# Seven block products in place of eight in the query/key and second gate projections of a two-block transformer kernel

## The chip, the cores and the metric

The kernel runs on one core of a Trainium2 chip, as one program. The metric is the device time of one execution in microseconds, the median over runs. A core has a matrix engine (TensorE, "PE"), a vector engine (VectorE, "DVE"), an activation engine (ScalarE, "ACT"), GpSimd ("POOL") and SyncE ("SP"), which here issues nearly all DMAs, in order, from one queue. All data is float32 unless a row says bf16.

## The reference

256 tokens of width 1024 pass a Conformer/SSM block with a convolutional FFN, and then a second block: adaptive RMSNorm, one input projection, two attentions, two gates, and a mixture of 32 experts. What the change touches is the second block's input projection and its users:

```python
h = rmsnorm(x, norm1_g[l]) * (1.0 + sc1[:, None, :]) + sh1[:, None, :]
proj = h @ w_in[l]
q_m, k_m, v_m, q_d, k_d, v_d, gate_m, gate_d = jnp.split(proj, IN_SPLITS, axis=-1)
qm = apply_rope(to_heads(q_m, MOBA_HEADS, MOBA_HEAD_DIM), cos_m, sin_m)   # k_m, q_d, k_d alike
...
merged = jax.nn.sigmoid(gate_m) * y_m + jax.nn.sigmoid(gate_d) * y_d
x = x + g1[:, None, :] * (merged @ w_out[l])
...
y_ffn = hierarchical_moe(h2, ...)        # 32 experts of 1024x512, 1024x512, 512x1024
```

q_m, k_m, q_d, k_d have 512 columns each (2048 together) and gate_m, gate_d 1024 each (2048 together). The other projections stay as they are.

## The kernel before

Weights stream from HBM in units of 512 columns (2 MB) into two buffers `dense[0]`, `dense[1]`, each used by turns (unit n goes to `dense[n % 2]`). A unit may be loaded once the unit two places before it is used up. PSUM has 8 banks; four of them (`NB = 4`) take the tiles of the projections in turn. A tile is 256 output columns for 256 tokens and fills a bank. PE opens a tile only when the tile four places before it has been read (`open_tile`, semaphore `tile_read`). The whole order is written out by hand: each engine has its own program, with semaphores between them, and an instruction that waits holds everything behind it on its engine.

The stages that matter here, in order:

1. FFN down, 8 units of 128 columns over 22 row chunks (L1019). SP loads the units one or two ahead of PE, with the last pieces of `w_ada` (L505), which DVE multiplies and sums.
2. Two norms (`norm("n2")`, `norm("r1")`). At the end DVE scales and ACT adds the bias chunk by chunk (`hT`, L1558), and PE follows the chunks. `keep_on` puts idle matmuls into the gaps.
3. The query/key stage ("qk"), 4 units, 8 tiles. A tile is 16 matmuls of 128x256 (2 halves of 128 columns, 8 chunks of 128 rows), all by `tile` (L769). ACT reads a tile with four copies of 32 partitions (rotated halves, L1565) and one whole copy (L1567). DVE then applies the rotary tables with three operations (L2177 to L2180).
4. The value stage ("v"), 2 units, 4 tiles (L1034).
5. Attention with the gate projection ("gate2", 4 units, 8 tiles) as filling: a loop of 16 steps `a`. A step has the scores of a pair of heads (L1048, in every odd step, issued ahead of the gate matmuls), 6 gate matmuls (L1096), three transposes of the probabilities (L1064), 2 gate matmuls, and after every odd step the products with v (L1081). DVE has `maxima(a + 1)` (L2141 to L2146) and `finish(a)` (L2152, L2156), ACT has `soften` (the exponential, L1576) and `move` (L1586, L1591). For an odd `a` below 8 the transposes wait for finish(a), which on DVE stands behind maxima(a + 1), which waits for the scores of this step.
6. A sum of squares (L1106), two output projections and `out2` (L769), routing, and the experts: 16 pairs, weights in a ring of nine 2 MB slots. Where a slot is still in use SP waits for its release. The first loads for the experts stand in SP's program between those of the projections.

A matmul of float32 is two records in the trace, so 16 matmuls are 32 records.

## Time and profile before

| | |
|---|---|
| median of 3 runs | 1346.85 us (1345.8 to 1349.13) |
| profiled execution, own time | 1348.95 us |
| its span | 1347.1 us |
| PE busy | 1319.4 us (98%) |
| DVE, ACT, POOL busy | 637.0, 270.8, 58.9 us |
| HBM read | 348.82 MB, 260 GB/s over the span |

How to read it: PE is busy almost always, so the first look is for stretches in which PE waits, and for what the wait is. The DMA engines are full in the last third only. Busy time of PE is modelled: matmuls overlap, so the length of a stretch of them is read from start to start, not from the mean duration. Lines are those of the kernel before.

### The profile page before, as it was taken

Reading aid. Unit: us, or ns where it says so; the run is one execution under the profiler, and the core shown is the slowest. Engines: PE = TensorE matmul, PEld = TensorE weight load, DVE = VectorE, ACT = ScalarE, POOL = GpSimd, SP = SyncE. Lnnn points to the kernel's source line nnn. Section 1 sums busy time; section 2 is a strip of 40 time slices with the busy share of each in tenths; the row PEclk is TensorE's granted clock in tenths of the full one; section 3 lists DMA queues with packets and bytes.
Section 4 is the critical chain, followed back from the end, with each engine's and each line's share of the span. In section 5 each row is a group of like instructions: output and inputs, shape, how many; then the busy total and the mean of one; then the engine's idle time right before and its main releaser. Section 6 shows DMA issues by size and latency. Waiting matters only on the chain.

```text
span 1347.1 us, 18147 instructions
## 1 busy us (share of the span) xinstructions
PE 1319.4 (98%) x6910; PEld 918.0 (68%) x6910; DVE 637.0 (47%) x1384; ACT 270.8 (20%) x566; POOL 58.9 (4%) x60
## 2 busy tenths in 40 slices
PE   9999999999999999999899999999999999999997
PEld 6888888888899888888685788854333433443332
DVE  4652389998426776720531455244333333332322
ACT  2311133220203000100442431033111111112112
POOL 0002112000000111100000000000000000000001
PEclk9999999999999999999999999999999999999999
DMA  7345333343447988767553344569999999999995
GB/s 270 126 153 160 108 126 127 126 141 125 167 146 267 323 300 308 228 192 262 226 181 131 126 188 168 207 227 414 419 423 427 427 428 428 427 427 428 425 422 218
DMA packets 122219, 350.93 MB, mean 261 GB/s; under 512 B 4768, under 2 KB 66464, under 8 KB 108704
## 3 DMA queue, kind: packets, MB, share of 16 engines
q1 hardware_dynamic: 120528, 348.68, 67.9%
q10 hardware_dynamic: 1616, 1.20, 0.3%
q8 instruction: 52, 0.85, 0.3%
q14 instruction: 23, 0.19, 0.0%
HBM read 348.82 MB, written 1.05 MB: 260 GB/s over the span
## 4 chain that ended last, share of the span: by engine, by line
PE 82%; DMA 7%; DVE 6%; issue 2%; ACT 1%; DVEq 1%; POOLq 0%; POOL 0%; SPq 0%; ACTq 0%
PE bank L769 38%; PE bank L1216 20%; PE bank L1019 6%; DMA arena<-in_w_gate 4%; PE bank L1096 4%; PE bank L1188 3%; PE bank L1306 2%; DVE arena L1881 2%; DMA dense<-in_w_gate 2%; PE bank L1034 2%; DVE scratch L1895 1%; PE bank L983 1%; PE bank L971 1%; PE bank L1048 1%; PE bank L822 0%
## 5 line engine op out<-in xcount | busy, mean ns | idle before, releaser
L769 PE MATMUL bank<-hT,dense 128*128 128x256 f32 x2048 | 446.0, 380 | 1.3 <-ACT hT L1407 0.8
L769 PEld LDWEIGHTS bank<-hT,dense 128*128 128x128 f32 x2048 | 388.5, 190 | 57.7 <-issue 6.3
L1216 PE MATMUL bank<-arena,scratch 128*64 128x512 f32 x864 | 228.0, 599 | 6.1 <-DMA arena<-in_w_gate 5.7
L1216 PEld LDWEIGHTS bank<-arena,scratch 128*64 128x64 f32 x864 | 71.0, 138 | 130.6 <-issue 118.5
L769 PE MATMUL bank<-arena,dense 128*128 128x256 f32 x704 | 154.6, 381 | 0.4 <-DVE arena L1957 0.4
L769 PEld LDWEIGHTS bank<-arena,dense 128*128 128x128 f32 x704 | 134.4, 191 | 20.1 <-issue 2.0
L1881 DVE SCALAR_TENSOR_TENSOR arena<-arena,par 128x256 f32<-128x256 f32 x240 | 97.8, 485 | 0.0
L2349 DVE TENSOR_TENSOR scratch<-scratch,bank 128x512 f32<-128x512 f32 x64 | 41.2, 684 | 92.1 <-PE bank L1306 90.7
L1216 PE MATMUL bank<-arena,hT 128*64 128x512 f32 x336 | 78.0, 596 | 0.7 <-ACT hT L1667 0.7
L1019 PE MATMUL bank<-region,dense 128*128 128x256 f32 x352 | 76.1, 379 | 0.0
L1019 PEld LDWEIGHTS bank<-region,dense 128*128 128x128 f32 x352 | 67.0, 190 | 9.0
L1216 PE MATMUL bank<-dense,scratch 128*64 128x512 f32 x160 | 70.6, 594 | 0.0
L2367 DVE SCALAR_TENSOR_TENSOR resid<-bank,lamp,resid 128x512 f32<-128x512 f32 x32 | 24.0, 750 | 94.3 <-PE bank L1216 94.3
L2056 DVE SCALAR_TENSOR_TENSOR arena<-arena 128x1024 f32<-128x1024 f32 x48 | 61.7, 1338 | 8.4 <-DMA arena<-in_w_ada 4.3
L1096 PE MATMUL bank<-hT,dense 128*128 128x256 f32 x256 | 61.0, 384 | 0.0
L2354 DVE TENSOR_TENSOR hT<-hT,bank 128x512 f32<-128x512 f32 x16 | 11.0, 687 | 99.6 <-PE bank L1216 99.6
L1216 PEld LDWEIGHTS bank<-arena,hT 128*64 128x64 f32 x336 | 24.2, 137 | 41.8 <-issue 40.0
L1096 PEld LDWEIGHTS bank<-hT,dense 128*128 128x128 f32 x256 | 46.6, 190 | 8.5 <-issue 3.3
L1654 ACT ACTIVATE scratch<-bank,small,gs 128x128 f32<-128x128 f32 x128 | 46.4, 474 | 3.9 <-PE bank L1188 3.9
L1663 ACT ACTIVATE hT<-bank 128x512 f32<-128x512 f32 x16 | 9.6, 597 | 181.4 <-PE bank L1216 181.4
L1188 PE MATMUL bank<-stat,region 128*128 128x128 bf16 x672 | 42.1, 219 | 0.0
L1819 DVE SCALAR_TENSOR_TENSOR arena<-bank,par,arena 128x255 f32 (+5 forms) x72 | 34.7, 481 | 9.6 <-DVE arena L1819 5.8
(355 smaller groups left out, 1173.9 us busy)
## 6 DMA issues: line engine op xcount, KB each, us to landing
dense<-in_w_in SPq DMA_DIRECT2D x23, 2048.0 KB, 8.2
arena<-in_w_gate SPq DMA_DIRECT2D x21, 2048.0 KB, 22.4
arena<-in_w_up SPq DMA_DIRECT2D x20, 2048.0 KB, 22.4
arena<-in_w_down SPq DMA_DIRECT2D x17, 2048.0 KB, 24.7
arena<-in_w_ada SPq DMA_DIRECT2D x12, 2048.0 KB, 8.1
dense<-in_w_ffn_up SPq DMA_DIRECT2D x22, 1024.0 KB, 7.7
dense<-in_w_down SPq DMA_DIRECT2D x8, 2048.0 KB, 28.9
arena<-in_w_up SPq DMA_DIRECT2D x14, 1024.0 KB, 23.7
```

Source lines behind the costliest of these rows:

```text
L769: last = mm(dst, chunk(k, m), src[:, k, :], start=k == 0, stop=k == k_n - 1)
L1019: last = mm(dst, w[:, k, :], act_t[:, k, :], start=k == 0, stop=k == KF - 1)
L1034: last = mm(b[:], hT[:, k, c * P:(c + 1) * P], w[:, k, :], start=k == 0, stop=k == KD - 1)
L1096: last = mm(b[:, m, :], w[:, k, (a % 4) * P:(a % 4 + 1) * P], hT[:, k, :], start=k == 0, stop=k == KD - 1)
L1188: last = mm(bank[m // 4][:, (m % 4) * 2 * CAP:(m % 4 + 1) * 2 * CAP], x[:, c, m * P:(m + 1) * P], s[:, r, c * 2 * CAP:(c + 1) * 2 * CAP], ...
L1216: last = mm(dst[e * CAP:(e + 1) * CAP, :], tokens(k, e), w[e][:, k, :], start=k == 0, stop=k == k_n - 1)
L1306: ins = mm(spread_bank[2 * half + c][:], selT[:, r, c * P:(c + 1) * P], x, start=n == 0, stop=n == 2)
L1654: f(xe[:, r, k * 2 * CAP:(k + 1) * 2 * CAP], bank[k // 4][:, (k % 4) * 2 * CAP:(k % 4 + 1) * 2 * CAP], ACT.Identity, scale=gs2[:, k:k + 1] ...
L1819: ins = stt(xbcT[:, at_j, s:T], src[:, :, 0:T - s], par_at("ssm_w", j * 4 + (3 - s)), xbcT[:, at_j, s:T], ALU.mult, ALU.add)
L1881: stt(conv_o[:, k, :], glu_v[:, k, ds(i, T)], par_at("conv_w", i + k * CK), conv_o[:, k, :], ALU.mult, ALU.add).then_inc(sem_("tap"), 1)
L2056: stt(w[:, m, :], w[:, m, :], 1.0, c_act, ALU.mult, ALU.mult, accum_out=mod[:, ds(turn * 8 + (4 * i + m), 1)]).then_inc(sem_("ada_summed"), 1)
L2349: tt(part, part, spread_bank[q][:], ALU.add).then_inc(sem_("y_added"), 1)
```

## The change

Each qk tile and each gate2 tile (2x2 blocks of the weight: 2 column halves of 128, 2 row halves of 512, and 2 token halves of 128) is computed by the Winograd form of Strassen's scheme: seven products of 4 matmuls of 128x128, 28 in place of 16 of 128x256. The products come in three groups: "first" p1, p3, p5, p6 (16 matmuls), "second" p7, p2 (8), "third" p4 (4), in the order first(t+1), second(t), third(t-1). They need

- sums of weight blocks per tile: 4 operations of 128x512, by DVE for qk (`weight_sums`), by POOL for gate2;
- four token sums of 128x512 once, by DVE after the norm, ahead of everything that DVE did there;
- fixes per tile: ACT copies two of the four products out of the bank (`copy_products`), DVE adds once or twice after each group (`fix_first`, `fix_second`, `fix_third`), and the result stands in the bank again, where ACT reads it as before.

A third weight buffer (slot 6 of the arena) is used for these ten units, so the load of unit n waits for unit n-3. Slots 0 and 1 now hold the sums, so the first two gate matrices of the experts and one down matrix are loaded after the last gate2 tile; the first qk unit is loaded among the FFN down units.

```diff
+FAST0, FAST1 = UNIT["qk"][0], UNIT["gate2"][0] + UNIT["gate2"][1]
+def buffer(n):
+    if FAST0 <= n < FAST1:
+        return (2, FAST0 % 2, 1 - FAST0 % 2)[(n - FAST0) % 3]
+    return n % 2
+SLOTS = {"p1": 0, "p3": 1, "p6": 2, "p5": 3, "p7": 2, "p2": 0, "p4": 2}
+BLOCK = {"first": ("p1", "p3", "p5", "p6"), "second": ("p7", "p2"), "third": ("p4",)}
...
@@ sync
                 load("down", u, lambda t: v3(t[:, 0:KF * P], P), wdn[:, :, u * P:(u + 1) * P])
                 if u < 2:
                     load_ada(10 + u)
+                if u == 1:
+                    load("qk", 0, flat, wi2[:, :, 0:512])
...
-            for e in range(2):
-                load_matrix("gate", e, 0)
-
+            load("qk", 1, flat, wi2[:, :, 512:1024])
+            load("qk", 2, flat, wi2[:, :, 1536:2048])
             sp.wait_ge(sem_("ada_summed"), 48)
             for e in range(2):
                 load_matrix("up", e, 0)
-            for u, c in enumerate((0, 512, 1536, 2048)):
-                load("qk", u, flat, wi2[:, :, c:c + 512])
+            load("qk", 3, flat, wi2[:, :, 2048:2560])
...
+            sp.wait_ge(tile_done, TILE["gate2", 7] + 1)
+            for e in range(2):
+                load_matrix("gate", e, 0)
             load_matrix("down", 1, 0)
@@ gpsimd
+            for t in range(NFAST):
+                n, j, tt = U0("gate2") + t // 2, t % 2, nc.gpsimd.tensor_tensor
...
+                tt(s1, a21, a22, ALU.add).then_inc(sem_("sums_ready"), 1)
+                pool.wait_ge(sem_("sums_ready"), before_t + 1)
+                tt(s2, s1, a11, ALU.subtract).then_inc(sem_("sums_ready"), 1)
+                pool.wait_ge(sem_("sums_ready"), before_t + 2)
+                tt(s4, a12, s2, ALU.subtract).then_inc(sem_("sums_ready"), 1)
+                tt(a21, a11, a21, ALU.subtract).then_inc(sem_("sums_ready"), 1)
@@ tensor
+            def fast(name, t, block, i0=0, i1=None, ready=None):
...
+                    if (block, i) == ("first", 0):
+                        open_tile(name, t)
+                        pe.wait_ge(sem_("sums_ready"), sums_count(name, t))
+                    if block == "second" and i == 0:
+                        pe.wait_ge(sem_("fast_fixed"), fast_count(name, "first", t))
+                    if block == "third" and i == 0:
+                        pe.wait_ge(sem_("fast_fixed"), fast_count(name, "second", t))
...
-            for u in range(4):
-                unit_512("qk", u, hT, ready=None if u else by_chunk("r1_out"))
+            fast("qk", 0, "first", 0, 8, ready=first_tokens)
+            fast("qk", 1, "first", 0, 8)
+            fast("qk", 0, "first", 8, 16, ready=first_tokens)
+            fast("qk", 1, "first", 8, 16)
+            for block, t in ORDER[2:]:
+                fast("qk", t, block)
...
-                some(0, 6)
-                attend(a, lambda: some(6, KD))
+                some(14 * a, 14 * a + 10)
+                attend(a, lambda: some(14 * a + 10, 14 * a + 14))
@@ scalar
+            for t in range(NFAST):
+                copy_products("qk", t)
+                if t >= 3:
+                    read_qk(t - 3)
...
@@ vector
+            for t in range(NFAST):
+                if t == 0:
+                    weight_sums("qk", 2)
+                fix_first("qk", t)
+                if t:
+                    fix_second("qk", t - 1)
+                    if t >= 2:
+                        fix_third("qk", t - 2)
+                    if t + 2 < NFAST:
+                        weight_sums("qk", t + 2)
+                if t == 1:
+                    unscale()
+                if t >= 4:
+                    rope(t - 4)
```

Where instructions stand now. SP's queue at the start of FFN down, before:

```order
L475 DMA dense1<-in_w_ffn_down 128x22x128 [waits tile_done]
L505 DMA arena<-in_w_ada_2 128x4x1024 [waits ada_summed]
L475 DMA dense0<-in_w_ffn_down 128x22x128 [waits tile_done]
L505 DMA arena<-in_w_ada_2 128x4x1024 [waits ada_summed]
L475 DMA dense1<-in_w_ffn_down 128x22x128 [waits down_unit]
L475 DMA dense0<-in_w_ffn_down 128x22x128 [waits tile_done]
```

and now (the last load but one is down unit 2):

```order
L537 DMA dense1<-in_w_ffn_down 128x22x128 [waits tile_done]
L567 DMA arena<-in_w_ada_2 128x4x1024 [waits ada_summed]
L537 DMA dense0<-in_w_ffn_down 128x22x128 [waits tile_done]
L567 DMA arena<-in_w_ada_2 128x4x1024 [waits ada_summed]
L537 DMA arena<-in_w_in_2 128x8x512
L537 DMA dense1<-in_w_ffn_down 128x22x128 [waits down_unit]
L537 DMA dense0<-in_w_ffn_down 128x22x128 [waits tile_done]
```

The first qk unit (`in_w_in_2`) went in front of down unit 2. ACT in the qk stage, before (tiles 0 and 1, in banks 3 and 0):

```order
L1565 ACTIVATE scratch1<-bank3 32x512 [waits tile_done,norm_ssq]
L1565 ACTIVATE scratch1<-bank3 32x512 x3
L1567 ACTIVATE region<-bank3 128x512
L1565 ACTIVATE scratch1<-bank0 32x512 [waits tile_done]
L1565 ACTIVATE scratch1<-bank0 32x512 x3
L1567 ACTIVATE region<-bank0 128x512
```

and now (L1701 is `copy_products` of tiles 0 to 4; bank3 holds tile 0 and then tile 4):

```order
L1701 ACTIVATE arena<-bank3 128x2x128 [waits fast_part,norm_ssq]
L1701 ACTIVATE arena<-bank0 128x2x128 [waits fast_part]
L1701 ACTIVATE region<-bank1 128x2x128 [waits fast_part]
L1701 ACTIVATE arena<-bank2 128x2x128 [waits fast_fixed,fast_part]
L1709 ACTIVATE scratch1<-bank3 32x512 [waits fast_fixed]
L1709 ACTIVATE scratch1<-bank3 32x512 x3
L1711 ACTIVATE region<-bank3 128x512
L1701 ACTIVATE arena<-bank3 128x2x128 [waits fast_fixed,fast_part]
```

The five reads of tile 0 went behind the copy of tile 3. PE in the qk stage, tiles 1 to 4, before (banks 0, 1, 2 and 3):

```order
L769 MATMUL bank0<-hT,dense1 128x256 x15
L769 MATMUL bank1<-hT,dense0 128x256 [waits tile_read1,dense_in0]
L769 MATMUL bank1<-hT,dense0 128x256 x15
L769 MATMUL bank2<-hT,dense0 128x256 [waits tile_read2]
L769 MATMUL bank2<-hT,dense0 128x256 x15
L769 MATMUL bank3<-hT,dense1 128x256 [waits tile_read3,dense_in1]
```

and from the end of tile 3's first group on, now (bank2 tile 3, bank1 tile 2, bank0 tile 1, bank3 tile 4):

```order
L910 MATMUL bank2<-arena 128x128 x8
L910 MATMUL bank1<-arena,dense1 128x128 [waits fast_fixed]
L910 MATMUL bank1<-arena,dense1 128x128 x3
L910 MATMUL bank1<-hT,dense1 128x128 x4
L910 MATMUL bank0<-arena 128x128 [waits fast_fixed]
L910 MATMUL bank0<-arena 128x128 x3
L910 MATMUL bank3<-hT,dense0 128x128 [waits sums_ready,tile_read3]
```

Twelve matmuls (rows two to six) now stand between the end of tile 3's first group and the opening of tile 4's bank; before there was nothing of tile 2 or 1 behind a tile's end, and a bank was opened a whole tile after its last reader could start.

## Rows read from the trace of the kernel before

**Rows 1.** The page: the chain that ended last, by engine.
```profile
PE 82%; DMA 7%; DVE 6%; issue 2%; ACT 1%; DVEq 1%; POOLq 0%; POOL 0%; SPq 0%; ACTq 0%
```
**Rows 2.** Windows: stretch, length, busy us of each engine, PEclk, DMA share, GB/s.
```profile
930.00:1312.00 382.00, 376.44 (x2274) 153.13 (x2272) 124.91 (x249) 61.62 (x155) 0.00 (x0) 1.00 1.01 425
```
**Rows 3.** Waits of PE: total us, times, longest.
```profile
PE bank L1216 <- DMA arena<-in_w_gate: 5.7, 4, 2.1
```
**Rows 4.** Timeline of PE, qk stage and start of v: start us, us, records.
```profile
658.74 55.49 PE L769 MATMUL bank<-hT,dense 128*128 128x256 f32 x256 [0.53 <-ACT hT L1558]
...
714.07 26.34 PE L1034 MATMUL bank<-dense,hT 128*128 128x512 f32 x61
```
**Rows 5.** Chain in order of time: start us, us; 128x128 matmuls, and FFN down.
```profile
416.47 10.50 PE bank L983 x94
...
565.10 75.97 PE bank L1019 x352
```
**Rows 6.** Timeline of SP, FFN down: issue of units 2 and 3.
```profile
574.63 9.86 SPq L475 DMA_DIRECT2D dense<-in_w_ffn_down  x2
```
**Rows 7.** Windows without engines: stretch, length, PEclk, DMA share, GB/s.
```profile
576.00:580.00 4.00, 1.00 1.11 306
580.00:584.00 4.00, 1.00 0.40 99
...
820.00:824.00 4.00, 0.58 1.06 397
```
**Rows 8.** Timeline of PE behind attention.
```profile
818.91 2.82 PE L1106 MATMUL bank<-scratch,con 128*128 128x256 f32 x8 [1.91 <-ACT scratch L1609]
```
**Rows 9.** Timeline of ACT, end of the norm and first qk tile.
```profile
658.09 3.30 ACT L1558 ACTIVATE hT<-hT,small 128x256 f32<-128x256 f32 x8 [2.40 <-DVE hT L2127]
665.98 2.43 ACT L1565 ACTIVATE scratch<-bank 32x512 f32<-32x512 f32 x4 [4.59 <-PE bank L769]
668.43 0.60 ACT L1567 ACTIVATE region<-bank 128x512 f32<-128x512 f32 x1
```
**Rows 10.** Timeline of DVE, the same stretch.
```profile
657.51 3.26 DVE L2127 SCALAR_TENSOR_TENSOR hT<-resid,gs,stat 128x256 f32<-128x256 f32 x8
660.69 1.74 DVE L2130 RECIPROCAL stat<-stat 128x256 f32<-128x256 f32 x1
662.46 2.50 DVE L2132 TENSOR_TENSOR resid<-resid,stat 128x512 f32<-128x512 f32 x4
668.54 0.69 DVE L2177 TENSOR_TENSOR stat<-scratch,con 128x512 f32<-128x512 f32 x1 [3.58 <-ACT scratch L1565]
```
**Rows 11.** Groups by shape: two DVE operations that read PSUM.
```profile
L2015 DVE TENSOR_SCALAR stat<-bank 128x128 f32<-128x128 f32 x2 | 0.6, 292 | 2.9 <-PE bank L993 2.9
L2100 DVE TENSOR_TENSOR resid<-bank,resid 128x256 f32<-128x256 f32 x1 | 0.4, 424 | 9.1 <-PE bank L1019 9.1
```
**Rows 12.** Timeline of PE in attention, steps 0 and 3.
```profile
746.18 0.55 PE L1064 MATMUL bank<-con,scratch 128*128 128x128 f32 x3 [0.84 <-DVE scratch L2156]
...
758.00 2.86 PE L1096 MATMUL bank<-hT,dense 128*128 128x256 f32 x12
760.69 0.49 PE L1064 MATMUL bank<-con,scratch 128*128 128x128 f32 x3
```
**Rows 13.** Timeline of DVE in step 3: end of finish(3).
```profile
759.79 0.67 DVE L2156 TENSOR_SCALAR scratch<-scratch,rsum 128x128 f32<-128x128 f32 x2
```
**Rows 14.** Groups by shape: POOL's operation of 128x512 on SBUF.
```profile
L708 POOL TENSOR_TENSOR arena<-arena 128x512 f32<-128x512 f32 x8 | 10.6, 1348 | 41.0 <-DVE arena L1920 41.0
```
**Rows 15.** Timelines: a DVE operation alone, one beside POOL's, which is last.
```profile
457.91 1.23 DVE L2056 SCALAR_TENSOR_TENSOR arena<-arena 128x1024 f32<-128x1024 f32 x1 [0.47 <-DVE scratch L2044]
459.06 1.74 DVE L2056 SCALAR_TENSOR_TENSOR arena<-arena 128x1024 f32<-128x1024 f32 x1
...
458.30 1.43 POOL L714 TENSOR_TENSOR region<-scratch 128x256 f32 x1 [5.42 <-ACT scratch L1515]
```
**Rows 16.** Timeline of SP behind attention.
```profile
836.44 14.18 SPq L475 DMA_DIRECT2D dense<-in_w_out  x2
```

More of the change, by code:

```diff
@@ L109, with user_before, fast_order, fast_count @@
 UNIT, NUNITS = offsets(UNITS)
+FAST0, FAST1 = UNIT["qk"][0], UNIT["gate2"][0] + UNIT["gate2"][1]
[3 more added lines that the diff above has]
+    return n % 2
+def user_before(n):
+    earlier = [m for m in range(n) if buffer(m) == buffer(n)]
+    return earlier[-1] if earlier else None
+SLOTS = {"p1": 0, "p3": 1, "p6": 2, "p5": 3, "p7": 2, "p2": 0, "p4": 2}
+BLOCK = {"first": ("p1", "p3", "p5", "p6"), "second": ("p7", "p2"), "third": ("p4",)}
+NFAST = 8
+def fast_order():
+    out = [("first", 0)]
+    for t in range(NFAST):
+        if t + 1 < NFAST:
+            out.append(("first", t + 1))
+        out.append(("second", t))
+        if t:
+            out.append(("third", t - 1))
+    return out + [("third", NFAST - 1)]
+ORDER = fast_order()
+FAST_COUNT = {x: i + 1 for i, x in enumerate(ORDER)}
+FAST_TILES = {"qk": 0, "gate2": NFAST}
+def fast_count(name, block, t):
+    return 3 * FAST_TILES[name] + FAST_COUNT[block, t]
+def part_count(name, block, t):
+    return 2 * FAST_TILES[name] + [x for x in ORDER if x[0] != "third"].index((block, t)) + 1
+def sums_count(name, t):
+    return t + (1 if t < 2 else 2) if name == "qk" else NFAST + 1 + 4 * (t + 1)
 HALVES = ("glu", "up")
@@ L159, in program @@
         up_slot, down_slot = [expert[2], expert[3]], [expert[4], expert[5]]
+        bufs = [dense[0][:], dense[1][:], expert[6]]
+        sum_sets = [[v3(arena[:, (3 * i + q) * 512:(3 * i + q + 1) * 512], P) for q in range(3)] for i in range(4)]
+        token_sums = [v3(arena[:, 6144 + 512 * q:6144 + 512 * (q + 1)], P) for q in range(4)]
         wdt = sb("wdt", KD * H)
@@ L1559, in _, with copy_products, read_qk @@
             act.wait_ge(sem_("norm_ssq"), norm_count("r1"))
-            for t in range(8):
-                b = wait_tile(act, "qk", t)
+            def copy_products(name, t):
+                act.wait_ge(sem_("fast_part"), part_count(name, "first", t))
+                if t >= 3:
+                    act.wait_ge(sem_("fast_fixed"), fast_count(name, "third", t - 3))
+                elif name == "gate2":
+                    act.wait_ge(sem_("fast_fixed"), fast_count("qk", "third", NFAST - 1))
+                f(fixes[t % 3][:, 0:4:2, :], v3(bank[TILE[name, t] % NB][:], P)[:, 0:4:3, :], ACT.Copy
+                  ).then_inc(sem_("fast_copied"), 1)
+            def read_qk(t):
+                b = bank[TILE["qk", t] % NB]
+                act.wait_ge(sem_("fast_fixed"), fast_count("qk", "third", t))
                 for to in range(0, P, 32):
@@ L2173, in _, with rope @@
             cos, sin = bc(con("cos"), 2), bc(con("sin"), 2)
-            for t in range(8):
+            def rope(t):
                 dst = qk[:, 2 * t:2 * t + 2, :]
```

184 lines of the change are left out of this document (146 added, 38 removed).

## The prediction

> **What bounds the kernel now.** I read four views, in this order. The chain of waits says that PE holds 82% of what ended last, DMA 7% and DVE 6% [rows 1]. PE's waits say where it isn't PE: the longest cause is the experts' gate matrices, 5.7 us in 4 waits [rows 3]. The windows say why: from 930 to 1312 us the DMA engines are full (share 1.01, 425 GB/s) while PE is at 376.4 of 382 us [rows 2]. So the last third is held by DMA and PE together, and it starts when the out2 tiles release their buffers. It gets neither shorter nor longer by this change, it only moves: a microsecond won or lost ahead of it is a microsecond of the whole. The timelines of the stages in front then show PE without a gap in qk [rows 4] and nearly so in attention, so fewer columns could pay there, one for one, if nothing else comes late.
>
> **What the products save.** The qk stage runs from 658.74 to 714.07, where v starts [rows 4]: 55.33 us for 8 tiles, 6.92 a tile of 16 matmuls. A 128x128 matmul is two records, and 94 such records with a weight load each take 10.50 us [rows 5], 0.2234 us a matmul. A tile of 28 costs 6.26 us, a stage of 8 tiles 50.0 us. That is 5.3 us less in qk and 5.3 us less in gate2.
>
> **qk, the start.** PE takes up the norm's output as ACT writes it, a chunk each 0.41 us until 661.39 [rows 9]. Before, a chunk met a matmul of 0.43 us. Now p1 and p3 want all eight chunks within 8 x 0.22 = 1.8 us and so end near 661.7, not 660.5. Eight matmuls of tile 1 follow, to 663.5; then p5 and p6 want the token sums. DVE is free at 660.77 [rows 10] and has four operations of 128x512 of 0.69 us, with a gap 0.73 each [rows 10], the second behind the last chunk: done near 663.7. PE goes on at 663.9. Together 16 matmuls took 5.1 us in place of 3.6: 1.5 us lost.
>
> **qk, tiles 4 to 7.** This is the step on which most rests. PE may open tile t+1 when ACT has read tile t-3. ACT reads it behind `copy_products(t)`, which waits for the first group of tile t. From the end of this group PE has 8 + 4 matmuls, 2.68 us. ACT needs 0.2 us to see it (a tile's last matmul ends at 658.74 + 6.92 = 665.66, and ACT starts 0.3 later), 0.3 for the copy until the next may start, 3.05 for the five reads of tile t-3 (665.98 to 669.03) [rows 9], and 0.1 back: 3.65 us. So PE waits 0.97 us at each of tiles 4, 5, 6 and 7: 3.9 us. Behind tile 7 the fix of its second group stands on DVE behind a rope of three operations (2.2 us); I count 0.9 us before the last p4. DVE's sum for the stage, by rows: weight sums 2.9 a tile (four of 0.73) for six tiles, fixes 1.9 (two of PSUM 128x256 at 0.42, four of 128x128 at 0.29 [rows 11], with gaps) for eight, the reciprocal and scaling 4.3 [rows 10], four ropes 2.2 each, token sums 2.9: 48.6 us, under PE's 56. The other four ropes go under v, whose 26 us hide them. Stage: -5.3 + 1.5 + 3.9 + 0.9 = +1.0 us. Bounds: -3.8 (only the start is lost) and +4.6 (rival C).
>
> **FFN down.** The first qk unit (2.1 MB) now stands in the queue in front of down unit 2. It has no wait of its own, so it is issued right behind the ada piece and before 574.63, when down unit 2 goes out [rows 6]. Before, the engines were full with the two until about 581.6 (share 1.11, then 0.40 of 4 us) [rows 7]. PE starts unit 2 at 565.10 + 2 x 9.50 = 584.1 [rows 5]: 2.5 us of cover. The new unit takes 2.1 MB / 425 GB/s [rows 2] = 4.9 us, so down 2 lands near 586.7 and PE waits 2.7 us. Later units have their 9.5 us each and no guest. The bounds are 0, and 4.5 at the 306 GB/s of the window before [rows 7]. On order: the Trainium skill, DMA: Bandwidth & Descriptors, "Queues, rings and completion order", says that SP owns one ring on each of the 16 DMA engines and that descriptors in it start in order; by that rule the guest is wholly ahead of down 2, by a fair sharing it would be so only in part. No row here separates the two.
> Does the clock fall? After 1.91 us idle it stood at 0.58 of 2.4 GHz for 4 us, that is mostly at 1.2 GHz [rows 7, 8]: 1.7 us lost. The idle times of up to 2.1 us among the experts left a mean of 1.00 over 382 us [rows 2, 3], so most of those had no fall. I take half, 0.9 us, with bounds 0 and 1.7.
>
> **gate2.** Of the 5.3 us not all arrives. A step has 10 matmuls of 0.223 ahead of the transposes where it had 6 of 0.432: PE comes 0.36 us earlier. In step 0 it already waits 0.84 us for DVE [rows 12]; it waits 0.36 more. In step 3 (and 1, 5, 7, which repeat it) finish(3) ends at 759.79 + 0.67 = 760.46 [rows 13] and the transposes start at 760.69 [rows 12], about 0.1 us after they could; both hang on scores that end at 758.00, so PE comes 0.27 us too early four times: 1.1 us. In even steps DVE has about 2 us of slack, of which the fixes of the odd step before take 1.3. From step 8 on there are 3 us. That leaves 3.8.
> The sums by POOL: 4 operations a tile, 1.35 us each [rows 14], 5.4 us a tile against 9 us of PE. Unit gate2-2 lands some 8 us after v's end and its first use is 31 us after it, so even twice the price is hidden. What is not hidden is what POOL does to DVE: the same operation took 1.74 us beside POOL and 1.23 alone [rows 15]. DVE's critical operations in the odd steps mostly read PSUM or one SBUF tensor; I take 0.4 us (bounds 0 and 4). Gate2 gains 3.4 us. The Trainium skill (GPSIMD Engine Reference, table of figures, "SBUF interfaces") says that POOL's ports are shared with VectorE and contend where DVE has two SBUF inputs; the trace agrees with 1.74 against 1.23.
>
> **Behind attention.** Gate2's last tanh no longer stands between the last product and the square; of its 0.6 us (like L1567 [rows 9]) I count 0.3 won. The idle time of 1.91 us thus becomes 1.6; whether the clock then stays up is open, up to 1.7 us won. I count none. Three matrices (6.3 MB) and down 0 are now loaded here, some 20 us with proj_d, from about 815; out2's load was issued at 836.44 [rows 16] with 14 us to its use at 850.6, so a queue that is full until 840 is hidden by the output projections.
>
> **Sum.** +1.0 +2.7 +0.9 -3.4 -0.3 = +0.9 us. The profiled execution took 1348.95 us for its span of 1347.1, so 1349.85 of its own kind; it lies 2.1 above the median of the runs (1346.85), so 1347.75, say 1347.8.
>
> **Rivals.**
> B, faster: the guest in the DMA queue is hidden (down 2 arrives by 584.1), the clock stays up behind attention, and the transposes aren't early. Then +1.0 - 4.9 (only step 0's 0.4 lost) - 0.3 - 1.7 = -5.9: 1341.0. For it: the cover is 2.5 us and the size of the guest's delay comes from a mean rate. Against: the DMA engines are full when the guest arrives, share 1.11 [rows 7].
> C, slower: DVE becomes the bound of qk. It has 48.6 us of work in 56; some 75 operations, each with a wait on its own semaphore. If each costs 0.15 us more than counted, DVE needs 59.9 and qk grows by 3.6: 1351.4. It decides from 0.1 us more per operation. Against: gaps of dependent operations before are 0.03 to 0.04 us.
> D, slower: in attention, POOL stretches DVE's chain between scores and transposes. If DVE's 2.5 us become 3.0 in all eight first steps, 4 us: 1351.8. It decides from 0.1 us, which is all the slack of the odd steps [rows 12, 13]. Against: POOL is at work in perhaps half of them.
> E, the products don't run at 0.2234 us: they read sums from other places and change groups often. At 0.236, 5.6 us more: 1353.4. Against: the 128x128 rows have loads for each as well.
>
> **Chances.** As forecast 0.50, with its own range 1344 to 1351; B 0.25, C 0.11, D 0.10, E 0.04. 0.3% (4 us) is about what a measurement of this kernel can tell from no change. Below 1342.8 lie most of B and a little of the forecast, 0.22; above 1350.9 most of C, D and E and a little of the forecast, 0.21; the rest, 0.57, between. The range of 1341 to 1354 leaves out a part of B and the case that two of C, D, E meet.
>
> **What would show it.** Four waits of PE of about 1 us each in the qk stage whose releaser is ACT's read (the last of five), and one on DVE before the last p4; a stage of 56 us. A wait of PE of 2 to 3 us on down unit 2, near 584. Waits of 0.2 to 0.4 us for L2156's successor at the transposes of steps 1, 3, 5, 7; an attention stage 3 to 4 us shorter. No wait of PE on POOL's sums, none on out2's weights, and the stretch from the first expert to the end as long as before. I am wrong if qk is under 53 us (ACT's read isn't the limit), if no wait stands near 584, or if the experts' stretch changes its length.

## The result, and the profile after

The changed kernel takes 1364.43 us (median of 4 runs, 1357.15 to 1365.09); the kernel before took 1347.86 us (4 runs) on the same chip. The ratio is 1.011, with a 95% interval of 1.008 to 1.014: slower, by more than the 0.3% that a measurement can tell, and 10 us above the end of the forecast's range. The profiled execution took 1364.54 us, its span 1362.7 us (before 1347.1): 15.6 us to account for.

The page's chain by engine, to be held against [rows 1], shows DVE up from 6% to 8% and ACT from 1% to 3%:

```profile
PE 81%; DVE 8%; DMA 5%; ACT 3%; issue 2%; DVEq 1%; POOLq 0%; POOL 0%; ACTq 0%
```

The window on the experts (stretch, length, busy us of each engine, PEclk, DMA share, GB/s), moved along by 13 us, and their longest wait of PE answer to [rows 2, 3]. The longest wait is 3.6 us where it was 2.1, but the sum is as before, and from the first product of the experts to the end the kernel takes 454.3 us (before 454.5): the loss lies ahead of them.

```profile
943.00:1325.00 382.00, 373.06 (x2258) 152.94 (x2270) 123.00 (x247) 63.14 (x156) 0.00 (x0) 1.00 1.01 424
```
```profile
PE bank L1348 <- DMA arena<-in_w_gate: 5.9, 3, 3.6
```

Three starts of stages (qk, v, the squares), read from the chain of waits, cut the span into parts. In the chain v starts 0.16 us later than in PE's timeline, so that qk before is 55.5 us here and 55.33 in the prediction. "att" is v and attention, up to the eight matmuls on the squares that stand behind attention [rows 8]; "rest" is what follows. All are us of one profiled execution.

```
kernel                          qk starts  qk length   att      rest    span
before                            658.7      55.5     104.7    528.2   1347.1
after                             667.4      57.1     111.9    526.3   1362.7
early unit in the kernel before   664.7      55.5     104.7    526.2   1351.0
unit behind all down units        666.2      57.1     108.8    526.5   1358.6
unit in four parts                658.9      57.1     107.9    526.2   1350.1
GpSimd's sums cut to 8 columns    664.3      57.1     100.4    525.7   1347.5
ScalarE reads first               664.8      54.6     111.9    526.7   1357.9
GpSimd additions in before        660.5      55.5     109.2    527.6   1352.8
sums on VectorE, late             667.5      57.1     117.8    528.0   1370.4
sums on VectorE, early            664.7      57.1     107.3    528.5   1357.6
 and both repairs                 660.5      54.6     109.5    528.1   1352.7
query/key products alone          659.2      54.5     104.7    526.7   1345.1
both repairs, sums released       660.8      54.7     101.5    526.7   1343.7
both repairs, sums not released   660.5      54.7     107.1    525.9   1348.2
```

After against before: +8.6 until qk starts, +1.6 in qk, +7.2 in attention, -1.9 behind it. Each row is one execution; a kernel's executions lie up to 8 us apart (the changed kernel's between 1357 and 1365).

PE's timeline after (start us, us, records, and in brackets the idle time before and what ended it) shows where PE waits. It answers to [rows 4, 8, 12].

```profile
588.00 4.61 PE L1142 MATMUL bank<-region,dense 128*128 128x256 f32 x10 [3.90 <-DMA dense<-in_w_ffn_down]
...
691.31 1.16 PE L910 MATMUL bank<-hT,dense 128*128 128x128 f32 x8 [0.87 <-ACT region L1711]
698.69 1.16 PE L910 MATMUL bank<-hT,dense 128*128 128x128 f32 x8 [0.86 <-ACT region L1711]
706.08 2.05 PE L910 MATMUL bank<-hT,arena 128*128 128x128 f32 x16 [0.87 <-ACT region L1711]
713.47 2.05 PE L910 MATMUL bank<-hT,arena 128*128 128x128 f32 x16 [0.87 <-ACT region L1711]
723.34 1.16 PE L910 MATMUL bank<-arena 128*128 128x128 f32 x8 [0.67 <-DVE arena L2277]
757.46 0.90 PE L1198 MATMUL bank<-con,scratch 128*128 128x128 f32 x3 [2.22 <-DVE scratch L2368]
766.27 0.55 PE L1198 MATMUL bank<-con,scratch 128*128 128x128 f32 x3 [2.50 <-DVE scratch L2368]
777.36 0.55 PE L1198 MATMUL bank<-con,scratch 128*128 128x128 f32 x3 [0.31 <-DVE scratch L2368]
808.49 1.50 PE L1215 MATMUL bank<-scratch,arena 128*128 128x256 f32 x4 [2.54 <-ACT scratch L1742]
836.42 1.99 PE L1238 MATMUL bank<-scratch,con 128*128 128x256 f32 x8 [1.56 <-ACT scratch L1767]
```

The wait at 588 and the qk stage look as forecast. What was not forecast is the size of the waits in attention: 7.6 us in four, where before it was 0.84 in one [rows 12]. The last of the four ends with ACT: its read of the product (L1742) stands behind its exponential, which had waited 7.0 us for DVE's L2358. The windows of 4 us add the clock. Below 1.00 in the third last column some or all of a window ran at 1.2 instead of 2.4 GHz:

```profile
584.00:588.00 4.00, 0.11 (x1) 0.03 (x1) 3.86 (x7) 0.00 (x0) 0.00 (x0) 0.85 1.17 291
588.00:592.00 4.00, 4.00 (x10) 3.20 (x11) 2.27 (x4) 0.00 (x0) 0.00 (x0) 0.50 1.10 274
...
652.00:656.00 4.00, 4.00 (x13) 3.26 (x12) 0.29 (x1) 2.56 (x6) 0.00 (x0) 0.62 1.10 425
756.00:760.00 4.00, 2.54 (x11) 2.32 (x11) 3.03 (x8) 1.22 (x4) 0.94 (x1) 0.68 0.86 318
...
768.00:772.00 4.00, 4.00 (x25) 3.40 (x22) 1.91 (x8) 1.64 (x6) 0.69 (x1) 0.61 0.02 4
808.00:812.00 4.00, 3.51 (x15) 3.34 (x16) 3.55 (x10) 2.41 (x9) 2.86 (x3) 0.58 0.00 0
836.00:840.00 4.00, 3.58 (x17) 3.17 (x18) 1.29 (x2) 3.34 (x6) 0.00 (x0) 1.00 1.06 442
```

Why is DVE late? Its timeline after, at the wait of 2.50 us and ahead of the one of 2.54, and POOL's beside it:

```profile
762.02 0.74 DVE L2357 TENSOR_REDUCE mx<-scratch 128x1 f32<-128x128 f32 x2
762.80 0.61 DVE L2358 TENSOR_SCALAR mx<-mx 128x2 f32<-128x2 f32 x1
...
763.51 2.70 DVE L2368 TENSOR_SCALAR scratch<-scratch,rsum 128x128 f32<-128x128 f32 x2
766.13 0.28 DVE L2268 TENSOR_TENSOR arena<-arena,bank 128x128 f32<-128x128 f32 x1
766.44 1.05 DVE L2270 TENSOR_TENSOR arena<-arena 128x128 f32<-128x128 f32 x1
767.42 0.55 DVE L2353 SCALAR_TENSOR_TENSOR scratch<-bank,con 128x384 f32<-128x384 f32 x1
...
801.54 2.91 DVE L2378 SCALAR_TENSOR_TENSOR scratch<-scratch,rsum 128x128 f32<-128x128 f32 x2
...
805.86 1.19 DVE L2358 TENSOR_SCALAR mx<-mx 128x2 f32<-128x2 f32 x1
```
```profile
762.12 1.27 POOL L806 TENSOR_TENSOR arena<-dense 128x512 f32<-128x512 f32 x1 [5.18 <-PE bank L910]
763.46 1.26 POOL L808 TENSOR_TENSOR arena<-arena,dense 128x512 f32<-128x512 f32 x1
764.80 1.26 POOL L810 TENSOR_TENSOR arena<-dense,arena 128x512 f32<-128x512 f32 x1
766.02 1.32 POOL L811 TENSOR_TENSOR dense<-dense 128x512 f32<-128x512 f32 x1
...
805.75 1.26 POOL L806 TENSOR_TENSOR arena<-arena 128x512 f32<-128x512 f32 x1 [0.17 <-POOL arena L811]
```

The pair that scales the probabilities took 0.67 us before [rows 13]; here 2.70. Its first half takes 1.29 us and ends at 764.80, just behind POOL's second operation (763.46 + 1.26), and its second half takes 1.37 and ends at 766.21, just behind POOL's third (764.80 + 1.26). L2358, two columns that take 0.17 us alone, takes 0.61 and ends at 763.41, POOL's first at 763.39. L2270 ends at 767.49, behind POOL's 767.34. Ahead of the wait at 808 it is the same: L2378 takes 2.91 us for two (0.84 without GpSimd's sums, experiment 3), L2358 1.19 beside POOL's 1.26. DVE's operations that read PSUM (L2268, L2353) or reduce (L2357) keep their times, and POOL's 32 take 1.26 to 1.32 us but for one of 1.46. So DVE is not slowed in proportion: some of its operations end only when POOL's whole operation is over. Of the 24 operations of the pair's line, 20 take 0.28 to 0.35 us and four 1.19 to 1.37, none between.

### The profile page after: what moved, and what is told of

Read it like the earlier page. It is cut to its first block, busy times and chain, and to the rows that moved or that the text cites. A ratio compares the mean times of both kernels' runs of the same rounds, so it can differ in the third digit from the quotient of the medians.

```text
span 1362.7 us, 19122 instructions
## 1 busy us (share of the span) xinstructions
PE 1317.0 (97%) x7279; PEld 929.4 (68%) x7294; DVE 695.9 (51%) x1500; ACT 276.4 (20%) x582; POOL 99.3 (7%) x92
## 4 chain that ended last, share of the span: by engine, by line
PE 81%; DVE 8%; DMA 5%; ACT 3%; issue 2%; DVEq 1%; POOLq 0%; POOL 0%; ACTq 0%
PE bank L858 34%; PE bank L1348 22%; PE bank L910 6%; PE bank L1142 5%; DMA arena<-in_w_gate 4%; PE bank L1320 3%; PE bank L1438 2%; DVE arena L2041 2%; PE bank L1168 2%; DMA dense<-in_w_ffn_down 1%; DVE scratch L2055 1%; PE bank L1106 1%; ACT scratch L1709 1%; PE bank L930 1%; PE bank L1094 1%
## 5 line engine op out<-in xcount | busy, mean ns | idle before, releaser
L858 PE MATMUL bank<-hT,dense 128*128 128x256 f32 x1792 | 390.5, 380 | 0.8 <-ACT hT L1539 0.8
L858 PEld LDWEIGHTS bank<-hT,dense 128*128 128x128 f32 x1792 | 339.3, 190 | 50.5 <-issue 4.9
L1142 PE MATMUL bank<-region,dense 128*128 128x256 f32 x352 | 79.2, 389 | 3.9 <-DMA dense<-in_w_ffn_down 3.9
L910 PE MATMUL bank<-arena 128*128 128x128 f32 x384 | 51.4, 283 | 0.7 <-DVE arena L2277 0.7
L910 PEld LDWEIGHTS bank<-arena 128*128 128x128 f32 x384 | 47.7, 198 | 1.9 <-DVE arena L2277 0.9
L782 POOL TENSOR_TENSOR region<-scratch 128x256 f32 (+1 forms) x22 | 23.2, 1054 | 277.1 <-ACT scratch L1647 277.1
L820 POOL TENSOR_TENSOR hT<-scratch,con 128x512 f32<-128x512 f32 x3 | 3.7, 1270 | 542.2 <-DVE scratch L2594 542.2
```

The lines of the kernel that those rows point to most:

```text
L858: last = mm(dst, chunk(k, m), src[:, k, :], start=k == 0, stop=k == k_n - 1)
L910: last = mm(b[:, SLOTS[p], :], left, right, start=k == 0, stop=k == 3)
L1142: last = mm(dst, w[:, k, :], act_t[:, k, :], start=k == 0, stop=k == KF - 1)
```

## The experiments

Ratios are to the kernel before, run anew beside each group of experiments (medians 1347.3 to 1348.4 us).

**1. The early unit, alone in the kernel before.**

```
+                if u == 1:
+                    sp.dma_start(flat(expert[6]), wi2[:, :, 0:512]).then_inc(sem_("guest_in"), 16)
...
+            sp.wait_ge(sem_("guest_in"), 16)
             load_matrix("down", 1, 0)
```

> The kernel before with one more load: the first query/key unit (2 MB) into an arena slot that is free there, issued by SP behind the last adaptive piece, ahead of FFN down unit 2, where the changed kernel issues it. Nothing else changes (the unit is loaded once more later, as before). Theory G (the early unit delays down unit 2, the PE waits, its clock falls, and the stage and the norm behind it run longer): query/key starts about 8.6 us later than in the kernel before (667.4 instead of 658.7), PE waits 3 to 4 us at about 588 for the down unit, total about 1355 to 1356. Rival N (the unit is absorbed, and the 8.6 us of the changed kernel came from its other instruction order): qk start within 1 us of 658.7, total 1347 to 1348.

Measured: 1352.83 us, ratio 1.0041 (1.0025 to 1.0056). PE's wait on the down unit, and the chain (start us, us, what):

```profile
PE bank L1022 <- DMA dense<-in_w_ffn_down: 3.8, 1, 3.8
```
```profile
574.78 13.17 DMA dense<-in_w_ffn_down
587.95 0.14 issue
588.08 58.90 PE bank L1022 x264
```

Theory G holds, but qk starts 5.9 us later, not 8.6, and the total is under the 1355 expected: 3.8 of waiting, and the six units behind it take 58.9 us instead of 57.0 because the clock falls (0.79 in 584:592). The other 2.7 of the changed kernel are a longer fall at the same place (60.0 us) and a second one in the norm. That one is no property of the change: PE idles 1.9 us there in every kernel, and the clock fell in the profiled executions of some kernels and not of others, whether or not they have the early unit (it did in experiments 5, 10, 11 and 12, and didn't before and in 1, 3, 4, 7, 8 and 9). Of this kernel's +5.9, 2.0 came back behind attention, where the clock stayed up after the same 1.9 us of idle time that it fell after before [rows 7, 8].

**2. The unit behind all down units.**

```
-                if u == 1:
-                    load("qk", 0, flat, wi2[:, :, 0:512])
...
+            load("qk", 0, flat, wi2[:, :, 0:512])
             load("qk", 1, flat, wi2[:, :, 512:1024])
```

> The changed kernel with the load of the first query/key unit moved behind all down units (SP issues it just before the second unit). Theory G: the wait at about 588 goes, query/key starts at 658 to 660 (667.4 in the changed kernel) if the unit is there in time, total 1364.4 - 8.6 = about 1356. Rival L (the unit now comes late for the query/key stage): a wait of PE of 1 us or more on that unit at the stage's start, total 1357 to 1361. Rival N (the order of instructions is the cause): start stays near 667, total 1363 to 1365.

Measured: 1360.98 us, 1.0092 (1.0072 to 1.0112); qk starts at 666.2. None of the three expectations holds as written; L comes nearest, with the total and a unit that is late, but late for DVE. The wait at 588 is gone, but another engine now waits for the unit; DVE's timeline:

```profile
634.94 0.69 DVE L2258 TENSOR_TENSOR arena<-arena 128x512 f32<-128x512 f32 x1 [50.29 <-DMA arena<-in_w_in]
```

`weight_sums("qk", 0)` stands ahead of the residual's additions in DVE's order. The additions start 5.6 us after the unit's arrival, PE waits 3.1 us at 644.6 for the norm's first input, and the clock is at 0.50 from 644 to 652. The unit has a window, then: it may not press on down unit 2, and it must be there by about 631.8, the 3.1 us of PE's wait earlier.

**3. GpSimd's sums cut to almost nothing.** This kernel forms only 8 columns of one plane of each sum of the gate units, so it leaves most of these sums out and its gates are wrong; the number, order and waits of all instructions stay.

```
                 s1, s2, s4 = sum_sets[t % 4]
+                a11, a12, a21, a22, s1, s2, s4 = (x[:, 0:1, 0:8] for x in (a11, a12, a21, a22, s1, s2, s4))
```

> The changed kernel with GpSimd's 32 weight sums of the second branch's gate units cut to 8 columns of one plane of each operand (so nearly all of these sums are left out, and the gates' products run on unsummed data; their number, order and waits stay). Theory C (VectorE's operations on the on-chip memory wait for a whole operation of GpSimd beside them, and PE then waits for VectorE at the probabilities and loses its clock): L2368's TENSOR_SCALAR pair falls back to about 0.67 us each at every head, the waits of 2.22, 2.50 and 2.54 us in the attention go or fall under 1 us, the granted clock in 758:774 and 808:812 rises to 0.9 or more, and the total falls by 7 to 11 us, to 1354 to 1357. Rival F (the fixes and copies of the block products themselves load VectorE and ScalarE too much there): durations fall but the waits stay at 1.5 us or more, total 1361 to 1364.

Measured: 1351.61 us, 1.0030 (1.0017 to 1.0042), so 13 us under the changed kernel, more than the 7 to 11 expected; attention 100.4 us, 11.5 less. The profiled execution also starts qk 3.1 us earlier, which GpSimd's sums can't have done, since they come later: the clock fell less ahead of qk here (58.9 us for the six units behind the wait, not 60.0, and 1.00 in the norm). DVE's groups (line, operation, shapes, count, busy us, mean ns), first here, then in the changed kernel:

```profile
L2369 DVE TENSOR_SCALAR scratch<-scratch,rsum 128x256 f32<-128x256 f32 x12 | 4.2, 353 | 0.4
L2369 DVE TENSOR_SCALAR scratch<-scratch,rsum 128x128 f32<-128x128 f32 x12 | 3.4, 287 | 0.4
```
```profile
L2368 DVE TENSOR_SCALAR scratch<-scratch,rsum 128x128 f32<-128x128 f32 x12 | 6.4, 530 | 0.4
L2368 DVE TENSOR_SCALAR scratch<-scratch,rsum 128x256 f32<-128x256 f32 x12 | 5.3, 438 | 0.4
```

Theory C. PE's waits of 2.22, 2.50, 0.31 and 2.54 shrink to one of 1.2 (step 0, where it was 0.84 before), and no window of attention has a clock under 1.00. The fixes and copies of the block products fit. Against before (104.7), the products themselves save 4.3 us here, 0.5 more than the forecast's 3.8.

**4. ScalarE reads before it copies.**

```
             for t in range(NFAST):
-                copy_products("qk", t)
                 if t >= 3:
                     read_qk(t - 3)
+                copy_products("qk", t)
```

> The changed kernel with ScalarE reading out tile t-3 of query/key before it copies the first products of tile t (now the copy comes first). Theory A (the four waits of 0.87 us in the query/key stage are PE waiting for ScalarE's readout that frees the bank): the four waits go or fall under 0.3 us, the stage shortens by about 3 us (57.1 to 54 us), total about 1361. Rival O (the copy then comes late and the waits move to the arena's or the fix's semaphore): the stage's length stays within 1 us, total 1363 to 1366.

Measured: 1356.43 us, 1.0058 (1.0041 to 1.0075). The four waits of 0.87 become one of 0.3; a new one of 0.8 on DVE's fix (L2268) appears, and and the one before the last p4 grows from 0.67 to 0.94; the stage is 2.6 us shorter (54.6 against 57.1). Theory A, with 0.8 lost again. The median fell by 8.0 us, of which the stage explains 2.6. The profiled execution, the slowest of the four, is 4.8 us under the changed kernel's; beside the stage, qk starts 2.6 us earlier in it, as the clock fell less ahead of it. What the other three won was not traced.

**5. GpSimd additions in the kernel before.** They work on a part of the arena that is free then; one load for the experts goes there later and now stands behind them in SP's queue. What follows attention takes 527.6 us (before 528.2), so this move cost nothing.

```
+            for ready, count in ((1, 8), (4, 4), (6, 4), (10, 8)):
+                pool.wait_ge(sem_("prob_ready"), ready)
+                for _ in range(count):
...
+                    nc.gpsimd.tensor_tensor(z, x, y, ALU.add).then_inc(sem_("extra"), 1)
```

> The kernel before with 24 GpSimd additions of 128x512 on a part of the arena that nothing else uses then (8 from the first probabilities on, 4 from the fourth, 4 from the sixth, 8 from the tenth), one memset ahead of them, and the second-branch experts' load into that part put behind them. VectorE's and TensorE's work is that of the kernel before. Theory C (an operation of VectorE on on-chip memory alone waits for GpSimd's whole operation): L2090s' TENSOR_SCALAR pairs beside GpSimd rise from 0.67 to 1.3 us or more each, PE waits more at the probabilities, and the attention (104.8 us from the first v product to the ossq products) lengthens by 3 to 9 us; total 1350 to 1356. Rival I (the changed kernel's fixes on VectorE are what leaves no slack, GpSimd alone is absorbed): VectorE's operations lengthen but the attention stays within 1.5 us, total 1346.5 to 1349.

Measured: 1354.93 us, 1.0057 (1.0041 to 1.0074); attention 109.2 us instead of 104.7, with every window in it at a clock of 1.00. Here neither products nor fixes are new, PE's work is untouched, and still the pair's means double or more (before 286 and 352 ns) while reductions (before 420) keep theirs, and POOL's operations take what they take elsewhere (1.26 to 1.28 us each). Of the pair's 24 operations 15 take 0.28 to 0.35 us and nine 1.21 to 1.37:

```profile
L2169 DVE TENSOR_SCALAR scratch<-scratch,rsum 128x128 f32<-128x128 f32 x12 | 8.4, 704 | 0.4
L2169 DVE TENSOR_SCALAR scratch<-scratch,rsum 128x256 f32<-128x256 f32 x12 | 8.3, 692 | 0.4
L2158 DVE TENSOR_REDUCE mx<-scratch 128x1 f32<-128x256 f32 x16 | 6.7, 420 | 0.6
```
```profile
L734 POOL TENSOR_TENSOR arena<-arena 128x512 f32<-128x512 f32 x24 | 30.4, 1268 | 55.8 <-DVE scratch L2169 34.5 <-DVE scratch L2179 19.8
```

Theory C again. The Trainium skill (SBUF — State Buffer, "SBUF: two separate sides") calls the port pair of VectorE and GpSimd an exclusive lock, which VectorE needs in a 2-port perf mode or with two SBUF inputs; whichever starts first holds it for its whole instruction while "the other fully blocks". The two groups of times above, with nothing between them, agree with it; no row tells the mode of an operation. My prediction had cited the contention for two SBUF inputs alone, and priced it as a slowdown; the entry of the Trainium skill that it cites (GPSIMD Engine Reference, "SBUF interfaces") names the 2-port perf mode too.

**6. All sums on VectorE, behind the first maxima.**

```
             maxima(0)
             finish(0)
+            for t in range(4):
+                weight_sums("gate2", t)
```

> The changed kernel with all weight sums of the gate units on VectorE instead of GpSimd (tiles 0 to 3 in the v stage, where VectorE idles 14 us; tiles 4 to 7 one to three operations behind the fixes of steps 2 to 11). Theory C: 32 operations of 0.7 us with none beside GpSimd: the attention takes 101 to 105 us instead of 111.9, total 1354 to 1358. Rival D (VectorE has no room for 16 more operations in the steps, 11.2 us beside 2.7 busy in 4.45): waits of PE on VectorE stay at 4 us or more in sum, attention 106 to 111 us, total 1359 to 1363.

Measured: 1370.27 us, 1.0160 (1.0139 to 1.0181), the slowest of all, and my own misplacement: `maxima(0)` can't start before v has ended, so the 16 operations didn't fall into DVE's 18.9 us of idle time but behind it, ahead of the maxima of the second step. PE's timeline:

```profile
759.46 3.76 PE L889 MATMUL bank<-hT,arena 128*128 128x128 f32 x16 [6.50 <-DVE arena L2243]
```

It says nothing on C or D; experiment 9 puts the order right.

**7. The unit in four parts.**

```
-                if u == 1:
-                    load("qk", 0, flat, wi2[:, :, 0:512])
+                if 2 <= u < 6:
+                    q = 2 * (u - 2)
+                    sp.dma_start(flat(bufs[2])[:, q:q + 2, :], wi2[:, q:q + 2, 0:512]).then_inc(dense_in[2], 16)
```

> The changed kernel with the first query/key unit loaded in four parts of 0.5 MB, one behind each of FFN down units 2 to 5, instead of 2 MB ahead of unit 2. Theory G (2 MB in one piece ahead of a 1.4 MB unit is what makes that unit late; 0.5 MB fits into the 2 us of slack of each): no wait of PE on a down unit, VectorE's first sums are done by about 620, query/key starts at 659 to 661, total 1356 to 1359. Rival E (VectorE, whose sums stand ahead of the residual's additions, is late again as with the unit behind all of them): query/key starts at 664 or later, total 1361 to 1364.

Measured: 1354.42 us, 1.0061 (1.0040 to 1.0082). No wait on a down unit, DVE's sums run from 611.6 to 617.2, and qk starts at 658.9, as before the change. Theory G, and the remedy costs nothing. Attention is 107.9 us here and 111.9 in the changed kernel with waits on the same lines (8.2 against 7.6 us in sum): every window of attention has a clock of 1.00 here. So of the 11.5 us that the contention costs in the changed kernel, some 7.5 (107.9 - 100.4) are waits, and 4 are clock falls behind them, which come in one execution and not in another. This split compares single executions: those of experiments 3 and 7 are the fastest of their kernels (1349.34 of a median of 1351.61, 1351.95 of 1354.42), that of the changed kernel is like three of its four. By the medians the sums cost 12.8 us (1364.43 - 1351.61), part of it clock ahead of attention.

**8. The block products in query/key alone**, with repairs 4 and 7; gates as before.

> The block products in query/key alone: the gates as in the kernel before (eight products per step, no GpSimd sums, no fixes), the first unit in four parts as in the run with that change alone, and ScalarE's readout ahead of its copy. Expected from the runs so far: query/key starts at 659 to 661 (before 658.7), lasts 54.6 us (before 55.3), attention 104 to 105 us, behind it as before or up to 0.8 us less: total 1346 to 1349, no measurable gain. Rival: the start of query/key costs more than its products save and the total is 1350 or more.

Measured: 1347.12 us, 0.9993 (0.9982 to 1.0003). As expected: 1.0 us of the stage (54.5 against 55.5) is all that is left of 5.3 us of products.

**9 and 10. Sums on VectorE, in its idle time where it has some**; 10 with repairs 4 and 7. Tiles 0 to 2 stand ahead of `maxima(0)`, the rest as one or two operations behind the fixes of a step:

```
+                for t, op in {1: [(3, 0)], 2: [(3, 1)], 3: [(3, 2), (3, 3)], 4: [(4, 0), (4, 1)],
...
+                              11: [(7, 0), (7, 1)], 12: [(7, 2), (7, 3)]}.get(a, ()):
+                    gate_sum(t, op)
```

> The changed kernel with the gates' weight sums on VectorE, tiles 0 to 2 ahead of the first maxima (VectorE idles there for 18.9 us in the run where they stood behind them), tile 3 to 7 one or two operations behind the fixes of each step from 1 to 12. Nothing on GpSimd. Theory P (what cost the last such run 6.5 and 2.9 us was only the place behind the first maxima): no wait of PE on the sums, v and attention together 101 to 105 us (111.9 with GpSimd, 100.4 with the sums left out), total 1350 to 1355. Rival D (20 more operations of 0.7 us in the steps leave VectorE no room): waits of PE on VectorE at the probabilities or of the bank over 3 us in sum, v and attention 106 us or more, total 1357 or more.

> The same with both other repairs: the first query/key unit in four parts of 0.5 MB behind down units 2 to 5 (query/key started at 658.9 with that alone), and ScalarE's readout ahead of its copy (stage 2.6 us shorter with that alone). Under P: the run without them less 5.5 to 8 us less 2.6 us, 1341 to 1346, faster than before. Under D: 1348 or more.

Measured: 1357.83 us, 1.0068 (1.0046 to 1.0090), and 1350.02 us, 1.0011 (1.0003 to 1.0020). Attention took 107.3 and 109.5 us, the second with two windows of a clock under 0.61. Rival D: without contention (the pair's operations all take 0.29 to 0.35 us), but with PE waiting for the last sum of tiles 5, 6 and 7. The waits of 9:

```profile
PE bank L889 <- DVE arena L2260: 4.0, 2, 2.0
...
PE bank L889 <- DVE dense L2260: 1.5, 1, 1.5
```

Whether a plan with these sums a step earlier would do was not tried.

**11 and 12. Both repairs, and the sums divided.** VectorE forms those of tiles 0 to 3, GpSimd those of 4 to 7: in 12 as soon as it can, in 11 each operation only at a moment that DVE names.

```
+                gates = {4: [('prob_ready', 3), ('prob_ready', 4), ('prob_ready', 5), ('prob_ready', 6)], ...
+                pool.wait_ge(sem_(gates[0][0]), gates[0][1])
                 tt(s1, a21, a22, ALU.add).then_inc(sem_("sums_ready"), 1)
```

> Both repairs; weight sums of gate tiles 0 to 2 on VectorE in the v stage, of tile 3 behind the fixes of steps 1 and 2, and of tiles 4 to 7 on GpSimd, each operation released by VectorE's own progress (mostly one operation of 1.27 us just after a head's probabilities are scaled, when VectorE has only short fixes and then a read of PSUM ahead). Theory C (contention costs only where a VectorE operation on on-chip memory alone stands beside GpSimd, and these moments have none that PE waits for): TENSOR_SCALAR pairs stay near 0.67 us, PE's waits at the probabilities under 1.5 us in sum, v and attention 100.5 to 103 us, total 1341 to 1344. Rival B (any GpSimd addition beside VectorE costs, wherever it stands): v and attention 105 us or more, total 1346 or more.

> The same without the releases: GpSimd forms the sums of tiles 4 to 7 as soon as unit and sum buffers are there, four operations back to back. Theory C: VectorE's TENSOR_SCALAR pairs beside them take 1.3 us or more, PE waits 2 us or more at a probability once or twice, v and attention 2 to 5 us longer than with the releases, total 1344 to 1348. Rival B: as long as with the releases, within 1 us.

Measured: 11 takes 1344.71 us, 0.9969 (0.9956 to 0.9982); 12 takes 1349.98 us, 1.0011 (1.0002 to 1.0021). Both lie above what was expected (1344 at most and 1348 at most), 11 by 0.7 us and 12 by 2. The same 16 GpSimd operations, moved by some microseconds, are worth 5.3 us of the whole (attention 101.5 against 107.1). DVE's pair in 11, then in 12:

```profile
L2390 DVE TENSOR_SCALAR scratch<-scratch,rsum 128x256 f32<-128x256 f32 x12 | 4.2, 353 | 0.4
L2390 DVE TENSOR_SCALAR scratch<-scratch,rsum 128x128 f32<-128x128 f32 x12 | 3.4, 286 | 0.4
```
```profile
L2385 DVE TENSOR_SCALAR scratch<-scratch,rsum 128x128 f32<-128x128 f32 x12 | 6.3, 528 | 0.4
L2385 DVE TENSOR_SCALAR scratch<-scratch,rsum 128x256 f32<-128x256 f32 x12 | 6.3, 524 | 0.4
```

Theory C; rival B falls. In 12 PE waits 2.04 us at a transpose and 2.54 at the second matmuls of a head; in 11 all waits of attention are 1.5 us in sum, 1.1 of them the one of step 0. In 12 the clock also fell once there (0.57 in 764:768), in 11 not. Version 11 is the fastest kernel of this study, 0.3% under the one before.

## Why the prediction was wrong

**The experts, the saving of the products, qk: right.** The last third only moved. The four waits on ACT's read came as 0.87 us each (forecast 0.97), the one before the last p4 as 0.67 (0.9); the stage grew by 1.6 us (forecast 1.0, bounds up to 4.6). From start to start such a tile takes 7.38 us (698.69 - 691.31), 1.1 more than its 28 matmuls, so the four cost 4.5 us, not 3.9: that is about the 0.6 between. Rival C of the prediction, DVE as the bound of qk, didn't come (a tile's fixes are three operations of 128x128, not the four that were counted), nor did E: 28 matmuls still take 6.3 us a tile.

**The step that failed: the price of GpSimd beside VectorE.** It stood in the sum as "I take 0.4 us (bounds 0 and 4)", with the argument that DVE's critical operations "mostly read PSUM or one SBUF tensor". It measured 11.5 us in the changed kernel (111.9 against 100.4), 7.5 without clock falls. Two things were wrong.

First, the only row on contention, 1.74 us beside POOL's 1.43 [rows 15], was read as a slowdown by some share. The trace of before held more. POOL's 1.43 is itself a held operation, and the DVE operation called alone ran beside it, until 459.06. Unhindered, the two take:

```profile
460.74 1.21 DVE L2056 SCALAR_TENSOR_TENSOR arena<-arena 128x1024 f32<-128x1024 f32 x1
```
```profile
466.35 0.72 POOL L714 TENSOR_TENSOR region<-scratch 128x256 f32 x1 [6.63 <-ACT scratch L1515]
```

POOL's began at 458.30 beside DVE's first and ended 0.67 us behind it, at 459.73; DVE's second, begun at 459.06, ended 1.07 behind that. Each waited for the other in turn. Of POOL's 22 operations of this line eleven take 0.72 or 0.73 us and eleven 1.28 to 1.43; of DVE's 44, 33 take 1.21 to 1.23 and eleven 1.74. Times in two groups are the sign of a hold; a shared rate would spread them. So a DVE operation of 0.29 us can take up to about 1.3 beside one of POOL's of 1.26.

Second, an operation with one tensor of SBUF was thought safe: the TENSOR_SCALAR pair is just that, it stands last ahead of PE's transposes, and it was hit most (11.7 us busy in place of 7.6). Rival D named the place and the engines, as a stretching and not as a hold, gave it 0.10 and priced it at 4 us above the forecast; it took "POOL is at work in perhaps half" of the steps as an argument against, where three waits of 2.2 to 2.5 us in a chain without slack [rows 12, 13] are enough. The rest of the gate2 term was sound: without the sums (experiment 3) the wait of step 0 is 1.20 us, 0.36 more than before as forecast; the four of 0.27 in the odd steps didn't come.

**The early unit: right place, too small.** Forecast 2.7 us of waiting and 0.9 of clock; measured alone 3.8 and 1.9, in the changed kernel 3.9 and 3.0. Down unit 2 landed 13.2 us after its issue, 1.2 us later than forecast: in the three windows until then (576 to 588) the engines moved 390, 342 and 291 GB/s at a share above 1.0, not 425. The forecast's own figures give 2.4 us (581.6 + 4.9 - 584.1) where it wrote 2.7. The 306 GB/s of the window before [rows 7] had been my upper bound (4.5 us), and was the nearer end. The further 1.7 us of the norm's clock fall were in no term; experiment 5 shows that fall (0.69 in 644:648) in a kernel without the early unit.

**Behind attention: better than forecast.** -1.9 instead of -0.3. The wait shrank from 1.91 to 1.56 as forecast and the clock stayed at 1.00, the gain that the prediction had left at "up to 1.7". But experiment 1 has it too, with the old wait of 1.9, so it isn't shown to come from the shorter wait.

By the forecast's terms, then: qk +1.6 (1.0), early unit and what follows +8.6 (3.6), attention +7.2 (-3.4), behind it -1.9 (-0.3): 15.5 against 0.9. Of the 14.6 between, 10.6 lie in attention: 11.1 in the one term of contention (11.5 for 0.4), less the 0.5 that the products saved more.

## What to carry to other kernels

Before work is put on GpSimd, list the VectorE operations on SBUF alone between two waits of the critical engine: here TENSOR_SCALAR and the operations with two SBUF tensors could be held for the whole of a GpSimd operation, whatever their own size, and reductions and reciprocals were not. If one stands there without slack, either release GpSimd by VectorE's own semaphores just behind it, or keep the operations off that stretch: here the same 16 operations differed by 5.3 us by their place. Look at single durations too, not at means: a held operation shows as a second group. And a load that is brought forward needs two checks, not one: what stands behind it in the DMA queue, and who waits for it in an in-order engine; cut into parts that fit the slack of each load it passes, it was free.

## What the runs showed of the hardware

- Beside GpSimd's TENSOR_TENSOR of 128x512 (1.26 to 1.28 us), VectorE's TENSOR_SCALAR with one SBUF source rose from 0.29 to 0.70 us in the mean of 12, single ones to 1.31, and its two-column form from 0.17 to 0.38 in the mean of 16 (experiment 5); TENSOR_REDUCE (0.42), RECIPROCAL of two columns (0.15 to 0.17) and operations with a PSUM source kept their times.
- GpSimd is held as well: its multiplication of 128x256 takes 0.72 us alone and 1.28 to 1.43 where VectorE's two-source operation of 1.2 us is running when it starts (eleven of 22, kernel before).
- A GpSimd addition of 128x8 took 0.20 us, and 32 of them left VectorE's means as they were without GpSimd (experiment 3).
- TensorE's clock: after 1.9 us idle in the norm it fell in some executions (0.69 in 644:648 of experiment 5) and stayed at 1.00 in others (before, same place); the four executions of the changed kernel had mean clocks of 0.990, 0.994, 0.990 and 0.990, and the second is the one 7 us shorter; after 2.5 us idle in attention it fell in the changed kernel and not in experiment 7. With idle times of about 2 us the fall is not settled by their length alone; what settles it stays open.
